# Differential attention stage: heads 0 and 1 normed inside the softmax loop and transposed in its drain

## The reference

```
def diff_branch(q, k, v, ..., subln_g, lambda_init):
    ...
    def block(i, qb):
        ...
        sc = jnp.einsum('bqchd,bkchd->bchqk', qb, k) + alibi[None, None]
        p = jax.nn.softmax(sc, axis=-1)
        a = p[:, 0] - lam * p[:, 1]
        return jnp.einsum('bhqk,bkhv->bqhv', a, v)
    o = sweep_query_blocks(block, q)
    o = rms_norm(o, subln_g) * (1.0 - lambda_init)
    return o.reshape(bsz, s, D_WIDTH).astype(dt)
...
merged = (g[:, :, 0] * (y_a @ w_up_a) + ... + g[:, :, 3] * (y_d @ w_up_d))
```

## Time and profile before

| | us |
|---|---|
| median of 3 runs | 2686.41 (2685.33 to 2687.3) |
| profiled execution, its own time | 2686.11 |
| its span | 2684.3 |
| PE busy | 2615.5 (97% of the span) |
| DVE busy | 1487.3 (55%) |
| ACT busy | 1125.5 (42%) |

### The profile page before, as it was taken

One profiled execution on the slowest core, in us unless ns is written; L12 is line 12 of the kernel. 1 busy time (PEld: TensorE's weight loads), 2 busy tenths in 40 slices (PEclk: granted clock), 3 DMA queues, 4 the chain that ended last, 5 costly groups with the idle time before them and its releaser, 6 DMA issues.

```text
span 2684.3 us, 34037 instructions
## 1 busy us (share of the span) xinstructions
PE 2615.5 (97%) x13218; PEld 2184.1 (81%) x13218; DVE 1487.3 (55%) x2761; ACT 1125.5 (42%) x1921; POOL 45.3 (2%) x69
## 2 busy tenths in 40 slices
PE   8998999999999999999999999999999999999998
PEld 6887778888888887788888787888888887788886
DVE  6756667554545567554444585644456485544444
ACT  3436454333645647232222344336446473322223
POOL 0000000000000000000000000000001000000000
PEclk9999999999999999999999999999999999999999
DMA  4220223123224321233333231233134221333332
GB/s 147 82 62 28 79 56 95 48 87 93 56 66 89 82 79 55 73 106 94 97 100 94 79 88 55 70 95 69 56 87 81 85 69 63 95 99 97 95 101 79
DMA packets 119007, 216.98 MB, mean 81 GB/s; under 512 B 14336, under 2 KB 21888, under 8 KB 118848
## 3 DMA queue, kind: packets, MB, share of 16 engines
q1 hardware_dynamic: 115104, 201.97, 24.9%
q0 software_dynamic: 3744, 12.85, 3.1%
HBM read 212.69 MB, written 2.10 MB: 80 GB/s over the span
## 4 chain that ended last, share of the span: by engine, by line
PE 88%; DVE 7%; ACT 3%; issue 2%; DMA 0%; SPq 0%; ACTq 0%; DVEq 0%
PE bank L571 41%; PE bank L574 29%; PE bank L714 6%; PE bank L703 3%; PE bank L683 2%; PE bank L684 2%; PE bank L743 1%; PE bank L760 1%; DVE wL L1435 1%; PE bank L614 1%; PE bank L797 1%; ACT wH L951 1%; DVE x L1500 0%; DVE hL L1514 0%; DVE gbuf L2080 0%
## 5 line engine op out<-in xcount | busy, mean ns | idle before, releaser
L1435 DVE TENSOR_TENSOR wL<-wraw,wH 128x1024 fp32r<-128x1024 f32 (+1 forms) x388 | 460.8, 1188 | 663.5 <-ACT wH L951 662.1
L951 ACT ACTIVATE wH<-wraw 128x1024 fp32r<-128x1024 f32 (+1 forms) x388 | 398.4, 1027 | 896.5 <-PE bank L571 481.5
L571 PE MATMUL bank<-wH,hH 128*128 128x512 f32 (+1 forms) x1248 | 500.5, 401 | 12.7 <-DVE wL L1435 7.3
L574 PE MATMUL bank<-hH,wH 128*128 128x512 f32 x1208 | 474.7, 393 | 3.9 <-ACT set L969 1.6
L571 PE MATMUL bank<-wH,hL 128*128 128x512 f32 (+1 forms) x1248 | 478.4, 383 | 0.0
L571 PE MATMUL bank<-wL,hH 128*128 128x512 f32 (+1 forms) x1248 | 478.1, 383 | 0.0
L574 PE MATMUL bank<-hL,wH 128*128 128x512 f32 x1208 | 470.9, 390 | 0.1
L574 PE MATMUL bank<-hH,wL 128*128 128x512 f32 x1208 | 470.7, 390 | 0.0
L571 PEld LDWEIGHTS bank<-wH,hH 128*128 128x128 f32 x1248 | 235.8, 189 | 68.8 <-DVE wL L1435 11.1
L571 PEld LDWEIGHTS bank<-wH,hL 128*128 128x128 f32 x1248 | 235.6, 189 | 48.0 <-issue 3.3
L571 PEld LDWEIGHTS bank<-wL,hH 128*128 128x128 f32 x1248 | 235.3, 189 | 47.9
(11 more groups left out here) (314 smaller groups left out, 2925.1 us busy)
## 6 DMA issues: line engine op xcount, KB each, us to landing
wraw<-in_w_in_dram SPq DMA_DIRECT2D x180, 512.0 KB, 3.6
wraw<-in_w_ffn_down_dram SPq DMA_DIRECT2D x44, 512.0 KB, 3.4
wraw<-in_w_ffn_gate_dram SPq DMA_DIRECT2D x40, 512.0 KB, 3.7
wraw<-in_w_ffn_up_dram SPq DMA_DIRECT2D x40, 512.0 KB, 3.6
wraw<-in_w_out_dram SPq DMA_DIRECT2D x24, 512.0 KB, 3.5
tab<-in_rpb_rev_dram POOLq DMA_DIRECT2D x32, 224.0 KB, 6.3
wraw<-in_w_up_a_dram SPq DMA_DIRECT2D x8, 512.0 KB, 3.4
wraw<-in_w_up_b_dram SPq DMA_DIRECT2D x8, 512.0 KB, 3.4
```

The source lines that it names most:

```text
L571: mm = pe.matmul(bank[t][:, 0:b.cols], act_part[:, k, t * P:(t + 1) * P], w_part[:, kk, :], start=first, stop=last)
L574: mm = pe.matmul(bank[b.bank0 + t][:, :], w_part[:, kk, t * P:(t + 1) * P], act_part[:, k, :], start=first, stop=last)
L951: A(wH[:, u % W_SLOTS, 0:width], wraw[:, u % RAW_SLOTS, 0:width], ACT.Copy).then_inc(S["w_hi"], 1)
L1435: V.tensor_tensor(wL[:, u % W_SLOTS, 0:width], wraw[:, u % RAW_SLOTS, 0:width], wH[:, u % W_SLOTS, 0:width].bitcast(F32), ALU.subtract).th ...
```

## The change

Heads 0 and 1 (a pair) are done with item 15, and now get their mean, root, reciprocal and scaling in steps 21 to 23 of the loop. Their transposes follow PE's steps 32 and 33, into banks 4 and 5, with ACT's and DVE's parts in the same steps. After the loop only heads 2 and 3 are normed; U30 starts with its first unit (heads 0 and 1), and PE transposes head 2 after the second group of that unit and head 3 after the third. ACT also takes a root of the constant one ahead of the second pair's root. The diff, with most of its context left out:

```diff
@@ -240,6 +240,7 @@
 DIFF_IDLE = (1, 3, 17, 19)
+Y_BANKS = (4, 5, 6, 7)
 FOX_IDLE = (0, 4, 8, 12, 16, 20, 24, 28)
@@ -599,7 +600,7 @@
 
-            def transposes(src, chunks, ready, count, each=0, halves=True):
+            def transposes(src, chunks, ready, count, each=0, halves=True, banks=None):
 
@@ -610,8 +611,9 @@
                         pe.wait_ge(S["tp_free"], i - TR_BANKS + 1)
+                    dst = bank[banks[k] if banks else SC + i % TR_BANKS]
                     for t in range(NT):
-                        mm = pe.transpose(bank[SC + i % TR_BANKS][:, t * P:(t + 1) * P], src[:, t, k * P:(k + 1) * P],
+                        mm = pe.transpose(dst[:, t * P:(t + 1) * P], src[:, t, k * P:(k + 1) * P],
                                           ident[:, :])
@@ -659,7 +661,7 @@
 
-            def softmax(items, v, side):
+            def softmax(items, v, side, drain=None):
 
@@ -714,6 +716,9 @@
                         mm.then_inc(S["pv_done"], 1)
+                    if drain and s in (len(items), len(items) + 1):
+                        pe.wait_ge(S["mx_done"], i0 + s - 1)
+                        drain(s - len(items))
 
@@ -905,9 +910,10 @@
                 evacuated(B("DV")[0])
-                softmax(diff_items(), v2, side_groups(B("G30", "G31"), done=1, idle=DIFF_IDLE))
-                transposes(ytok, 4, "y_ready", 0, each=1)
-                dense(L, "U30", 4)
+                def head(h):
+                    transposes(ytok, (h,), "y_ready", 0, each=1, banks=Y_BANKS)
+                softmax(diff_items(), v2, side_groups(B("G30", "G31"), done=1, idle=DIFF_IDLE), head)
+                dense(L, "U30", 2, each={(0, 1): lambda: head(2), (0, 2): lambda: head(3)})
                 dense(L, "U31", each={(1, 0): lambda: transposes(merged, (0, 1), "y_ready", NT),
@@ -1373,12 +1379,20 @@
                 dense(L, "G30", between=lambda i: [diff_rows(2), diff_rows(3)], stop=1)
-                softmax(diff_items(), side_groups(B("G30", "G31"), done=1, idle=DIFF_IDLE), q2, k2)
-
-                act.wait_ge(S["ms_ready"], n("ms_ready"))
-                A(st32[:, 0:16], st32[:, 0:16], ACT.Sqrt).then_inc(S["sd_ready"], 1)
-                hi_chunks(4, yH, lambda k: g_sub[l])
-                dense(L, "U30")
+                def head_roots(pair):
+                    act.wait_ge(S["ms_ready"], n("ms_ready"))
+                    ms = st32[:, 0:16].rearrange("p (t h) -> p t h", h=4)[:, :, 2 * pair:2 * pair + 2]
+                    A(ms, ms, ACT.Sqrt).then_inc(S["sd_ready"], 1)
+
+                def early_heads(s):
+                    if s == 21:
+                        head_roots(0)
+                    elif s in (32, 33):
+                        hi_chunks((s - 32,), yH, lambda k: g_sub[l], Y_BANKS)
+                softmax(diff_items(), side_groups(B("G30", "G31"), done=1, idle=DIFF_IDLE), q2, k2, early_heads)
+                A(one_col, one_col, ACT.Sqrt)
+                head_roots(1)
+                dense(L, "U30", between=lambda i: hi_chunks((2, 3), yH, lambda k: g_sub[l], Y_BANKS) if i == 0 else None)
                 dense(L, "U31", between=lambda i: hi_chunks((0, 1, 2, 3), hH, lambda k: 0.5) if i == 1 else None)
@@ -2235,18 +2249,42 @@
                 dense(L, "G30", between=lambda i: [diff_rows(2), diff_rows(3)], stop=1)
-                softmax(l, diff_items(), side_groups(B("G30", "G31"), done=1, idle=DIFF_IDLE), q2, k2)
-                dve.wait_ge(S["y_squared"], 4 * NT * (l + 1))
-                V.tensor_scalar(st32[:, 0:16], st32[:, 0:16], 1.0 / P, EPS, ALU.mult, ALU.add).then_inc(S["ms_ready"], 1)
-                dve.wait_ge(S["sd_ready"], n("sd_ready"))
-                then(V.reciprocal(st32b[:, 0:16], st32[:, 0:16]))
-                then(V.tensor_scalar(st32b[:, 0:16], st32b[:, 0:16], 1.0 - lambda_init(l), None, ALU.mult))
-                for h in range(4):
+                def by_pair(z, pair):
+                    return z[:, 0:16].rearrange("p (t h) -> p t h", h=4)[:, :, 2 * pair:2 * pair + 2]
+
+                def head_means(pair):
+                    dve.wait_ge(S["y_squared"], 4 * NT * l + 2 * NT * (pair + 1))
+                    ms = by_pair(st32, pair)
+                    V.tensor_scalar(ms, ms, 1.0 / P, EPS, ALU.mult, ALU.add).then_inc(S["ms_ready"], 1)
+
+                def head_scales(pair):
+                    dve.wait_ge(S["sd_ready"], n("sd_ready"))
+                    then(V.reciprocal(by_pair(st32b, pair), by_pair(st32, pair)))
+                    r = by_pair(st32b, pair)
+                    then(V.tensor_scalar(r, r, 1.0 - lambda_init(l), None, ALU.mult))
+
+                def scaled_head(h):
                     z = ytok[:, :, h * P:(h + 1) * P]
                     V.tensor_tensor(z, z, r, ALU.mult).then_inc(S["y_ready"], 1)
-                lo_chunks(4, yH, yL, lambda k: g_sub[l])
-                dense(L, "U30", merge(L, 3, 0))
+
+                def early_heads(s):
+                    if s == 21:
+                        head_means(0)
+                    elif s == 22:
+                        head_scales(0)
+                        scaled_head(0)
+                    elif s == 23:
+                        scaled_head(1)
+                    elif s in (32, 33):
+                        lo_chunks((s - 32,), yH, yL, lambda k: g_sub[l], Y_BANKS)
+                softmax(l, diff_items(), side_groups(B("G30", "G31"), done=1, idle=DIFF_IDLE), q2, k2, early_heads)
+                head_means(1)
+                head_scales(1)
+                for h in (2, 3):
+                    scaled_head(h)
+                dense(L, "U30", merge(L, 3, 0),
+                      lambda i: lo_chunks((2, 3), yH, yL, lambda k: g_sub[l], Y_BANKS) if i == 0 else None)
                 dense(L, "U31", merge(L, 3, 1),
```

## The result

Over nine runs each, the changed kernel takes 2692.23 us (2689.61 to 2696.16) and the kernel before 2686.41 us (2685.05 to 2690.56). The ratio is 1.0022, with a 95% interval of 1.0012 to 1.0032: 5.8 us slower, at least 3 and at most 9. That is inside the forecast range (2683.5 to 2693.5), on the forecast side, and 2.3 us above the forecast of 2689.9.

What follows compares the result with a forecast made beforehand. PE, busy 97% of the span, was taken as the bound. Per layer, 3.0 us lost in the middle, less drain gains of 1.1 and 2.2, plus 0.4 of clock, gave +3.5: 2689.9 us, range 2683.5 to 2693.5.

Steps and rivals of the forecast that it cites:

- The wait at score 24: Middle of the loop: DVE's wait for item 15's Square delays the row split, so PE stalls 2.2 us per layer.
- The rest of the middle: After score 24: 0.6 us more at item 25's transposes behind ACT's table loads, 0.2 for later latencies, per layer.
- The drain: From score 31 to U30's second unit: gains 1.1 us in the first layer, 2.2 in the second; low clock costs 0.4 each.
- The waits forecast ahead of PV 30 and PV 31: Drain: PE waits 1.5 to 2.5 us for DVE's scaling; the PE, ACT, DVE, PE round trip twice costs 3.7 us.
- Head 2's transposes: In U30's first unit, after two groups, PE waits 1.56 us for the second pair's norm.
- The row at 246 to 256.3 us: Profile row cited for low clock with PE half busy: 7.54 of 10.3 us busy, mean clock 0.67.
- the 1.1 us of low clock: Second layer's first U30 unit took 6.67 us against 5.57; the change was to regain that difference.
- The idle goes as intended: Rival, 9%: first unit covers the second pair's norm and the middle has room; 11.7 us less, 2674.7.
- The middle is covered: Rival, 14%: no loss in the loop's middle, drain as forecast; -2.5 us, 2683.9; needs item 15's Square about 2 us earlier.
- ACT's detour is longer: Rival, 10%: each table switch holds ACT twice the load's 1.28 us, exponential 22 later; +2.2 us, 2692.1.
- The clock falls in the drain and holds: Rival, 18%: low clock before PV 30 costs 2.1 us instead of 0.4; +3.3 over both layers, 2693.2.
- The sum: Whole kernel: +2.3 us in the first layer, +1.2 in the second, together +3.5; median forecast 2689.9.

Runs made afterwards that it cites:

- experiment 1: Kernel before, plus only a DVE wait in step 21 for the Square of item 15: 2692.33 us, ratio 1.0022.
- experiment 4: Changed kernel with DVE's low parts of heads 0 and 1 one step later, in steps 33 and 34: 2684.89 us, ratio 0.9992.
- experiment 2: Kernel before, plus one root of the constant one on ACT in step 21, bringing two table loads: 2690.61 us, ratio 1.0018.
- experiment 3: Changed kernel with the old drain: all four heads transposed, copied and split after the loop, before U30 starts: 2694.61 us, ratio 1.0032.
- experiment 5: Changed kernel with first pair's mean and root in step 22, scales in 24, heads 0 and 1 in 24 and 25: 2688.43 us, ratio 1.0008.
- experiment 6: Changed kernel with first pair's mean in step 24, root in 29, scales in 30, heads 0 and 1 in 30 and 31: 2685.19 us.
- experiment 7: Changed kernel with both the late norm (root in step 29) and the low parts one step later: 2676.41 us, ratio 0.9958.
- experiment 8: Changed kernel with late norm, later low parts, and ACT's root of the constant one moved to step 33: 2675.81 us, ratio 0.9956.

## Why the prediction was right, and where it was off

**The wait at score 24** (2.2 us forecast): right. It is 1.96 us of idle time, 2.1 us in distance, in both layers, and experiment 1 shows that the wait behind the Square alone makes it. DVE's idle time was forecast at 2.7 us and was 2.65.

**The rest of the middle** (0.8 us): too small. It was 1.6 and 1.2 us. In the second layer the mechanism was right: ACT's two loads make the transposes of item 25 late by the 0.6 us forecast,

```profile
2218.09 0.63 PE L705 MATMUL bank<-ident,sbufS 128*128 128x128 f32 x4 [0.65 <-DVE sbufS L1659]
```

and the short gaps around them came to 0.6 us instead of the 0.2 allowed. In the first layer PE did not wait there at all, because the low clock had made it late already. What the step left out is the clock. I had looked for a fall only in the drain, and in the first layer one came behind the stall of 2 us in the middle of dense work:

```profile
1038.00:1042.00 4.00, 2.04 (x8) 1.34 (x8) 3.89 (x11) 3.27 (x6) 0.00 (x0) 0.96 0.40 131
1042.00:1045.50 3.50, 3.50 (x11) 2.76 (x10) 2.49 (x8) 3.08 (x6) 0.00 (x0) 0.56 0.00 0
1072.00:1076.50 4.50, 4.39 (x16) 3.85 (x17) 0.69 (x3) 2.33 (x8) 0.00 (x0) 0.62 0.02 4
```

PE was busy for all of 1042 to 1045.5 at a mean clock of 0.56. Experiment 1, which has no loads, gives its price as 1.6 us (20.26 against 18.60 and against 18.63 in its own second layer). The fall followed in four of the eight places that have this stall and in none of the twelve without it, so that the two belong together is likely. Why it comes after one stall and not after its like is not shown; no run here settles it.

**The drain** (a gain of 1.1 us in the first layer and 2.2 in the second, less 0.4 of clock each, so 0.7 and 1.8): the mechanism was right. 0.7 and 2.5 us were measured. The waits forecast ahead of PV 30 and PV 31 (the chain had PV 31 3.7 us later; it came 3.6 later after score 31) were 1.68 and 2.11, and experiment 4 shows their cause by taking 1.68 and 1.81 us of them away with a change of order alone. The clock fell in the first layer's drain (0.62 from 1072 to 1076.5, PV 31 with 1.81 us instead of 1.13) and not in the second's. It put the second unit 0.65 us later in the first layer than in the second, a mean of 0.3 where 0.4 each was taken. Head 2's transposes waited 0.17 and 1.10 us, for 1.56 forecast: where the clock was low the two groups filled the gap, as forecast. Two things in this part of the prediction were not as it has them. The row at 246 to 256.3 us, read as PE half busy, has PE busy for 73% of the stretch. And the 1.1 us of low clock that the second layer was to give back are no property of that layer: in kernels with the old drain and the same code behind it the first unit took 5.57 and 6.67 us (before), 6.65 and 6.63 (experiment 1), 5.83 and 6.22 (experiment 2).

Taken over all profiles, the clock fell in the drain or right behind it in eight of eight places with the old drain (before, experiments 1 to 3), in three of six with the drain of the change (the change, experiments 5 and 6), and in none of six with the low parts one step later (experiments 4, 7 and 8).

**The rivals.** "The idle goes as intended" did not come about, for the two reasons named against it; experiment 7 shows that the idea itself is sound, since it gives 10 us once both are mended. "The middle is covered" is where experiment 6 arrives (2685.19, 2683.9 forecast), by moving the norm later and not the Square earlier. "ACT's detour is longer" is refuted by experiment 2, where exponential 22 starts 2.9 us after the end of exponential 21, where the forecast had 2.8. "The clock falls in the drain and holds" was not what happened in this profile, but a fall in another place cost 1.6 us, half of what the rival had over both layers (3.3 us there, 3.4 by its own terms).

**The sum.** 3.5 us were forecast; 3.9 us were measured in the stages of the profiled executions, and 5.8 us by the medians (3 to 9 by the interval). That the first two agree to 0.4 us is in part luck: the middle cost 7.1 us where 6.0 were forecast, the drain gained 3.2 where 2.5 were, and the two errors offset each other. Of the 10 us by which the profiled execution of the change is longer than that of before, 3.9 had come about ahead of score 18 of the first layer and 1.8 between the first layer's second unit and the second layer's score 18. In the second of these stretches the clock fell to a mean of 0.76, in a stage that the change does not touch:

```profile
1520.00:1527.00 7.00, 5.92 (x22) 4.42 (x23) 6.22 (x11) 5.20 (x9) 0.00 (x0) 0.76 0.24 75
```

Such a fall between 1500 and 1540 us stands in the profiles of the change and of experiment 6 and in none of the other eight. Across the ten profiles score 18 of the first layer stands between 1022.3 and 1027.8 us, with the same instructions ahead of it. Whether the 1.9 us between 3.9 and 5.8 are more falls of the clock or chance is left open; the interval holds both.

The forecast chance of 0.30 for slower by over 0.2% was low for what came: 0.22%, just above that bound. With the fall of the clock after the stall in the sum (0 to 1.6 us a layer) it would have stood nearer to one half, by my estimate.

## What to carry to other kernels

In an engine's written order, ask of each inserted instruction not only what it costs but what stands behind it: a mean of 0.17 us cost 2 us because it waited, ahead of a row split that PE needed, for a Square behind 2.8 us of copies on ACT; and a low part that nobody needed yet cost waits of 1.7 and 2.1 us by standing ahead of a scaling on a round trip. Put such work in the steps where both engines are seen idle, and behind what the bounding engine waits for next. Two table loads of 1.28 us each cost 2.0 us a layer where ACT had no slack, and 0.3 to 0.5 us eight steps later.

## What the runs showed of the hardware that was not expected

- A stall of PE of 1.9 to 2.0 us amid otherwise full work can be followed by a stretch at 1.2 GHz (0.68, then 0.83 mean clock in experiment 1; 0.56 in the change), worth up to 1.6 us: almost as much as the stall. It came in four of eight equal places, and in none of twelve without the stall.
- ACT's table load runs ahead of the wait of the instruction it serves: in the kernel before it started at 1063.05, as soon as the last Square's result was read, while DVE's mean, which the root waits for, ran from 1063.06 to 1063.24:

```profile
1063.06 0.18 DVE L2240 TENSOR_SCALAR small<-small 128x16 f32<-128x16 f32 x1 [0.47 <-ACT set L1105]
```

  So a root of a constant right ahead of a waiting root hides nothing. In the change, where it stands there, the load again starts right behind the last Square and the waiting root follows the load's end:

```profile
1074.95 1.28 ACT L1393 ACT_TABLE_LOAD   x1
...
1076.36 0.20 ACT L1385 ACTIVATE small<-small 128x8 f32<-128x8 f32 x1
```

  To hide the load it has to stand ahead of the work before it; that gave 0.5 us of the 1.28 in experiment 8.
